# Encoder layer on one core: neighbourhood-attention scores as 64x64 products on the four quarters of the array

## What is computed

```python
s = jnp.einsum('bnqhd,brnchd->bhnqrc', qr, kr).astype(jnp.float32) * scale
bias = jnp.take(col_bias, row_off, axis=1).transpose(0, 2, 3, 1, 4)
s = jnp.where(mask, s + bias.astype(jnp.float32), -jnp.inf)
p = jax.nn.softmax(s.reshape(s.shape[:4] + (-1,)), axis=-1)...
o = jnp.einsum('bhnqrc,brnchd->bnqhd', p, vr)
```

## Time and profile before

| | |
|---|---|
| median of 3 runs | 1249.09 us (1248.29 to 1249.78) |
| profiled execution | 1249.72 us, its span 1248.2 us |
| PE busy | 1172.1 us (94% of the span) |
| DVE, ACT, POOL busy | 649.2, 468.8, 265.6 us |
| granted TensorE clock, mean | 0.977 |

### The profile page before, as it was taken

One profiled execution on the slowest core, in us unless ns is written; L12 is line 12 of the kernel. 1 busy time (PEld: TensorE's weight loads), 2 busy tenths in 40 slices (PEclk: granted clock), 3 DMA queues, 4 the chain that ended last, 5 costly groups with the idle time before them and its releaser, 6 DMA issues.

```text
span 1248.2 us, 18969 instructions
## 1 busy us (share of the span) xinstructions
PE 1172.1 (94%) x6758; PEld 951.7 (76%) x6758; DVE 649.2 (52%) x1244; ACT 468.8 (38%) x982; POOL 265.6 (21%) x384
## 2 busy tenths in 40 slices
PE   6999999999998999999999999999994999999955
PEld 5888888878886777888889788768684888887732
DVE  6332232311114788433367564655466998885247
ACT  6322222200104667211225333445323667674223
POOL 3222222200002223001101000000004233554344
PEclk9999999999998999999999999999996999999978
DMA  9573443763129412442214001732598899979966
GB/s 312 136 239 118 119 159 109 250 158 73 34 56 225 113 27 78 148 158 94 84 25 133 2 1 68 249 121 103 201 346 304 319 386 340 374 291 357 403 263 242
DMA packets 112268, 225.26 MB, mean 180 GB/s; under 512 B 39862, under 2 KB 52158, under 8 KB 112062
## 3 DMA queue, kind: packets, MB, share of 16 engines
q1 hardware_dynamic: 88942, 168.64, 40.8%
q0 software_dynamic: 17856, 43.02, 10.3%
q10 hardware_dynamic: 5392, 12.59, 3.0%
HBM read 180.89 MB, written 69.78 MB: 201 GB/s over the span
## 4 chain that ended last, share of the span: by engine, by line
PE 81%; DVE 5%; DMA 4%; issue 3%; ACT 3%; SPq 2%; POOL 1%; DVEq 0%; ACTq 0%; POOLq 0%
PE bank L565 17%; PE bank L567 17%; PE bank L566 16%; PE bank L2294 5%; PE bank L2070 4%; PE bank L2222 3%; PE bank L2092 3%; PE bank L2260 2%; PE bank L2079 2%; PE bank L2016 2%; PE bank L2231 2%; PE bank L2156 1%; DMA at<-y_mix 1%; PE bank L2280 1%; DVE at L560 1%
## 5 line engine op out<-in xcount | busy, mean ns | idle before, releaser
L565 PE MATMUL bank<-at,at 128*128 128x512 f32 (+1 forms) x1192 | 442.3, 371 | 5.9 <-DVE at L560 3.4
L567 PE MATMUL bank<-at,at 128*128 128x512 f32 (+1 forms) x1192 | 431.8, 362 | 0.0
L566 PE MATMUL bank<-at,at 128*128 128x512 f32 (+1 forms) x1192 | 431.0, 362 | 0.0
L565 PEld LDWEIGHTS bank<-at,at 128*128 128x128 f32 x1192 | 226.1, 190 | 40.6 <-DVE at L560 3.9
L567 PEld LDWEIGHTS bank<-at,at 128*128 128x128 f32 x1192 | 225.7, 189 | 35.2
L566 PEld LDWEIGHTS bank<-at,at 128*128 128x128 f32 x1192 | 226.2, 190 | 32.3
L560 DVE TENSOR_TENSOR at<-at,at 128x1024 fp32r<-128x1024 f32 (+2 forms) x162 | 181.6, 1134 | 86.7 <-ACT at L555 84.0
L555 ACT ACTIVATE at<-at 128x1024 fp32r<-128x1024 f32 (+2 forms) x162 | 154.4, 988 | 146.7 <-DVE at L1529 47.5
L894 POOL TENSOR_TENSOR at<-at 128x1 f32<-128x1 f32 x88 | 24.7, 281 | 501.7 <-ACT at L1259 282.2
L2294 PE MATMUL bank<-at,at 128*128 128x512 f32 x156 | 74.2, 597 | 3.3 <-ACT at L1333 3.3
L1006 POOL DMA_INDIRECT y_tok<-at,at x39 | 39.5, 1013 | 132.5 <-DVE at L1867 95.9
(11 more groups left out here) (214 smaller groups left out, 1409.6 us busy)
## 6 DMA issues: line engine op xcount, KB each, us to landing
at<-in_w_exp_gate SPq DMA_DIRECT2D x39, 512.0 KB
at<-in_w_exp_up SPq DMA_DIRECT2D x39, 512.0 KB
at<-in_w_exp_down SPq DMA_DIRECT2D x39, 512.0 KB
at<-y_tok SPq DMA_DIRECT2D x24, 512.0 KB, 9.7
at<-in_w_in SPq DMA_DIRECT2D x6, 1024.0 KB, 11.3
xT_hi_all<-at POOLq DMA_DIRECT2D x12, 512.0 KB, 3.9
xT_lo_all<-at POOLq DMA_DIRECT2D x12, 512.0 KB, 5.7
at<-xT_hi_all SPq DMA_DIRECT2D x3, 2048.0 KB, 12.0
```

Of the source, the lines that this page charges most:

```text
L565: nc.tensor.matmul(out, w_hi, x_hi, start=(k == 0), stop=False)
L566: nc.tensor.matmul(out, w_lo, x_hi, start=False, stop=False)
L567: last = nc.tensor.matmul(out, w_hi, x_lo, start=False, stop=(k == len(terms) - 1))
```

## The change

- Scores: for each of the two column blocks and each of the two heads one product of 64 queries, 64 rows deep, read straight from `qk`: four products a step instead of two, of the same 256 or 384 columns of keys. The rows used are the head's (half of the array's rows), the output partitions the column block's (half of its columns). A bank now holds one head, and its two halves the two blocks. Only the last product of a bank counts up `s_done`.
- No `q_diag`, no zeroing, no POOL copies, no wait for them. `qk` holds the queries in the order that the products want: the copies out of PSUM write them with a stride of 4 elements (`channel_chunk`). ACT's and DVE's loops over channel tiles are written out, since tiles differ.
- `values`: the loops over block and head swap places; the count of products and their sizes stay.
- Bias tables: a partition now belongs to a column block and needs both heads: 2 heads x 2 kinds x 12 x 32 numbers for each pair. A head takes 16 DMAs instead of 8, each of 2 kinds instead of 3. Heads 0 to 2 are spread ahead of `channel_tiles(1)`, heads 3 to 5 behind it, heads 6 and 7 (their tables take the place of pair 1's, after a memset on POOL) during pair 2, eight DMAs after each of the stores of groups 0 to 3. DVE waits for six heads ahead of pairs 0 to 2, for all eight ahead of pair 3.
- Stores of the attention: two DMAs a group as before, split by column block instead of by head, in runs of 128 numbers instead of 64.
- `FINAL_ORDER` is another permutation; `BY_DVE`'s order comes out the same.

The diff without its context lines (left out too: renumbered counts, the loops written out, the wait for the copies moved):

```diff
-FINAL_ORDER = (0, 4, 1, 5, 2, 6, 3, 8, 7, 10, 9, 11)
+FINAL_ORDER = (0, 4, 5, 1, 6, 2, 8, 3, 10, 7, 11, 9)
...
-        na_bias = at(96, NPAIR, 3, KREL, KC)
-        na_bias_row = at(114, NPAIR, 3, KREL, KC)
+        na_bias = [at(kb, 2, 2, KREL, KC) for kb in (96, 108, 120, 108)]
+        na_bias_row = [at(kb + 6, 2, 2, KREL, KC) for kb in (96, 108, 120, 108)]
...
-        q_diag = [at(132 + 2 * j, 4, 2, QC, QROWS) for j in range(2)]
-        na_o = [at(136 + j, 4, HD) for j in range(2)]
+        na_o = [at(136 + j, 2, 2, HD) for j in range(2)]
...
-        def first_then_loop(eng, n, body):
-            body(0)
-            with eng.Fori(1, n) as i:
-                body(i)
+        def channel_chunk(tile, n, x):
+            out = qk[:, tile, n * CH:(n + 1) * CH]
+            if tile >= NPAIR:
+                return out, x
+            return (out.rearrange("p (g n c r) -> p g r n c", n=4, c=QC, r=QROWS),
+                    x.rearrange("p (g r n c) -> p g r n c", n=4, c=QC, r=QROWS))
...
-            def spread_bias(h):
-                for qr in range(QROWS):
-                    rows = slice((h % 2) * HD + qr, (h % 2 + 1) * HD, QROWS)
-                    src = bias_src[h * QC:(h + 1) * QC]
-                    sp.dma_start(na_bias[rows, h // 2], src[:, :, 3 - qr:15 - qr]).then_inc(bias_here, 16)
-                    sp.dma_start(na_bias_row[rows, h // 2, :, qr:qr + 8], src[:, :, 3:11]).then_inc(bias_here, 16)
+            def spread_bias(h, qr):
+                src = bias_src[h * QC:(h + 1) * QC]
+                for n in range(2):
+                    rows, kinds = slice(n * HD + qr, (n + 1) * HD, QROWS), slice(n, n + 2)
+                    sp.dma_start(na_bias[h // 2][rows, h % 2], src[:, kinds, 3 - qr:15 - qr]).then_inc(bias_here, 16)
+                    sp.dma_start(na_bias_row[h // 2][rows, h % 2, :, qr:qr + 8], src[:, kinds, 3:11]).then_inc(bias_here, 16)
...
-            for h in range(NH // 2):
-                spread_bias(h)
+            for h in range(3):
+                for qr in range(QROWS):
+                    spread_bias(h, qr)
-            for h in range(NH // 2, NH):
-                spread_bias(h)
+            for h in range(3, NH - 2):
+                for qr in range(QROWS):
+                    spread_bias(h, qr)
...
             def store_group(hp, g):
-                for half in range(2):
-                    dst = y_mix[g * GTOK:(g + 1) * GTOK, bass.ds(HALF + (2 * hp + half) * HD, HD)]
-                    sp.dma_start(dst.rearrange("(n q) d -> q n d", n=4),
-                                 na_o[g % 2][half * HD:(half + 1) * HD]).then_inc(na_stored[g % 2], 16)
+                dst = y_mix[g * GTOK:(g + 1) * GTOK, HALF + hp * P:HALF + (hp + 1) * P].rearrange("(s n q) d -> n q s d", s=2, n=2)
+                for n in range(2):
+                    sp.dma_start(dst[n], na_o[g % 2][n * HD:(n + 1) * HD].rearrange("p s h d -> p s (h d)")).then_inc(na_stored[g % 2], 16)
             def head_pair(hp):
...
-            with sp.Fori(1, NPAIR - 1) as hp:
-                head_pair(hp)
+            head_pair(1)
+            sp.wait_ge(pool_made, MADE_LAST_BIAS)
+            for g in range(NKG):
+                store_group(2, g)
+                if g < QROWS:
+                    for h in range(NH - 2, NH):
+                        spread_bias(h, g)
...
-            pool.memset(na_bias_row, MASKED).then_inc(pool_made, 1)
-            for j in range(2):
-                pool.wait_ge(qk_done[j], NH // 2)
-            for j in range(2):
-                pool.memset(q_diag[j], 0.0).then_inc(pool_made, 1)
-            pool.wait_ge(pool_made, MADE_ZERO)
-            for j in range(2):
-                pool.wait_ge(qk_evac_v[j], 2 * (NH // 2))
-                pool.wait_ge(qk_evac_s[j], NH // 2)
-            def head_pair(hp):
-                for g in range(NKG):
-                    pool.wait_ge(s_done, 2 * (NSTEP * hp + max(2 * g - 2, 0)))
-                    for half in range(2):
-                        rows = slice(half * HD, (half + 1) * HD)
-                        q = qk[rows, hp, g * GTOK:(g + 1) * GTOK].rearrange("p (r n c) -> p n c r", n=4, c=QC)
-                        pool.tensor_copy(q_diag[g % 2][rows, :, half], q).then_inc(diag_ready, 1)
-            first_then_loop(pool, NPAIR, head_pair)
+            for hp in range(NPAIR - 1):
+                pool.memset(na_bias_row[hp], MASKED).then_inc(pool_made, 1)
+            pool.wait_ge(s_biased, 2 * 2 * NSTEP)
+            pool.memset(na_bias_row[NPAIR - 1], MASKED).then_inc(pool_made, 1)
-            pool.wait_ge(diag_ready, 2 * NPAIR * NKG)
...
-                        nc.vector.tensor_copy(qk[:, 2 * i + j, n * CH:(n + 1) * CH], bank[3 * j + n][:]).then_inc(qk_evac_v[j], 1)
+                        nc.vector.tensor_copy(*channel_chunk(2 * i + j, n, bank[3 * j + n][:])).then_inc(qk_evac_v[j], 1)
-            with dve.Fori(1, NH // 2 - 1) as i:
+            for i in range(1, NH // 2 - 1):
-            dve.wait_ge(bias_here, 32 + 16 * 3 * QC + 16 * 2 * NH * QROWS)
             def head_pair(hp):
+                dve.wait_ge(bias_here, 32 + 16 * 3 * QC + 16 * 4 * QROWS * (NH if hp == NPAIR - 1 else NH - 2))
                 def scores(s):
-                    bias = (na_bias_row if row_masked else na_bias)[:, hp, kind:kind + 2, first:first + width // KC].rearrange("p n r c -> p n (r c)")
+                    bias = (na_bias_row if row_masked else na_bias)[hp][:, :, kind, first:first + width // KC].rearrange("p h r c -> p h (r c)")
...
-                    o = bank[6 + s % 2][:, 0:P].rearrange("p (n d) -> p n d", n=2)
+                    o = bank[6 + s % 2][:, 0:P].rearrange("p (h d) -> p h d", h=2)
-                    nc.vector.tensor_tensor(na_o[g % 2][:, 2 * (s % 2):2 * (s % 2) + 2], o, r, ALU.mult).then_inc(o_evac, 1)
+                    nc.vector.tensor_tensor(na_o[g % 2][:, s % 2], o, r, ALU.mult).then_inc(o_evac, 1)
...
-                    if s % 2 == 0:
-                        pe.wait_ge(diag_ready, 2 * (NKG * hp + g + 1))
+                    row0 = keys[0] * QROWS
-                        q = q_diag[g % 2][:, block].rearrange("p h c r -> p (h c r)")
-                        row0 = keys[0] * QROWS
-                        k = qk[:, NPAIR + hp].rearrange("p (r c) -> p r c", c=GW)
-                        k = k[:, row0:row0 + QROWS * len(keys), COL_START[block]:COL_START[block] + KC]
-                        nc.tensor.matmul(bank[2 * (s % 2) + n][:, 0:P * len(keys)], q, k, start=True, stop=True).then_inc(s_done, 1)
+                        for half in range(2):
+                            rows = slice(half * HD, (half + 1) * HD)
+                            q = qk[rows, hp, g * GTOK + block * HD:g * GTOK + (block + 1) * HD]
+                            k = qk[rows, NPAIR + hp].rearrange("p (r c) -> p r c", c=GW)
+                            k = k[:, row0:row0 + QROWS * len(keys), COL_START[block]:COL_START[block] + KC]
+                            mm = nc.tensor.matmul(bank[2 * (s % 2) + half][n * HD:(n + 1) * HD, 0:P * len(keys)], q, k, start=True, stop=True)
+                            if n == 1:
+                                mm.then_inc(s_done, 1)
...
-                    for n in range(2):
+                    for half in range(2):
-                            for half in range(2):
-                                rows = slice(half * HD, (half + 1) * HD)
-                                last = nc.tensor.matmul(bank[6 + s % 2][rows, n * HD:(n + 1) * HD],
-                                                        na_pT[s % 2][:, n, k * P + half * HD:k * P + (half + 1) * HD],
+                            for n in range(2):
+                                last = nc.tensor.matmul(bank[6 + s % 2][n * HD:(n + 1) * HD, half * HD:(half + 1) * HD],
+                                                        na_pT[s % 2][:, half, k * P + n * HD:k * P + (n + 1) * HD],
...
```

More of the change, by code:

```diff
@@ L253, in hymba_encoder @@
         pool_made, fill_made = (sem(n) for n in ("pool_made", "fill_made"))
-        MADE_CONST, MADE_BIAS, MADE_ZERO, MADE_ROUTE = 4, 6, 8, 21
+        MADE_CONST, MADE_BIAS, MADE_LAST_BIAS, MADE_ROUTE = 4, 8, 9, 22
         x_sq, x_rs, xs_ready, xt_done = (pair(n) for n in ("x_sq", "x_rs", "xs_ready", "xt_done"))
@@ L267, in hymba_encoder @@
         hi_made, lo_made = sem("hi_made"), sem("lo_made")
-        diag_ready, s_done, s_biased, p_exp, s_rcp = (
-            sem(n) for n in ("diag_ready", "s_done", "s_biased", "p_exp", "s_rcp"))
+        s_done, s_biased, p_exp, s_rcp = (sem(n) for n in ("s_done", "s_biased", "p_exp", "s_rcp"))
         pt_done, pt_evac_s, pt_evac_v, o_done, o_evac = (
@@ L1151, in channel_tiles @@
                     act.wait_ge(qk_done[j], i + 1)
-                    nc.scalar.activation(qk[:, 2 * i + j, CH:2 * CH], bank[3 * j + 1][:], ACT.Copy).then_inc(qk_evac_s[j], 1)
+                    nc.scalar.activation(*channel_chunk(2 * i + j, 1, bank[3 * j + 1][:]), ACT.Copy).then_inc(qk_evac_s[j], 1)
```

(9 more changed lines are left out.)

## The result

The changed kernel takes 1257.29 us (median of 4 runs, 1256.55 to 1258.94), beside 1248.69 for the kernel before in the same comparison: a ratio of 1.0074, with a 95% interval of 1.0055 to 1.0093. So it is slower, by 0.74%. The forecast was 1252.7 us and slower, a loss of 3.6 us; the loss is 8.6.

What follows compares the result with a forecast made beforehand. PE, with 81% of the chain, was taken to bound the kernel; +10.9 -3.2 -3.3 +4.0 -3.3 +2.0 -3.5 makes +3.6 us on the profiled 1249.7, 1253.3, less 0.6 to the median: 1252.7 us, range 1240 to 1266.

Steps and rivals of the forecast that it cites:

- channel stage: Second pair of channel tiles: 48 bias DMAs at 0.64 us delay its weights on SP; +10.9 us with 0.5 for the clock.
- pair 0: Attention's start: PE's wait for POOL's copies shrinks, but values wait for `v_att`; the pair gains only after it, -3.2 us.
- pair 1: Attention: nine of twelve iterations gain from shorter score passes, 5 x 0.27 + 4 x 0.48, so -3.3 us.
- pair 2, wait at pair 3, clock: Last 32 bias DMAs behind stores make SP slower and DVE start pair 3 late, +4.0 us; PE's low clock after, +2.0.
- between attention and final stage: Everything between these stages follows PE and shifts with it; no term of its own.
- final stage: DVE fills its 4.86 us wait for tile 1's root, and tile 9 is last instead of 11: -3.5 us (bounds -4 and 0).
- Rival A: Bias DMAs issue faster, at 0.52 us, and the kernel is faster: 1241.9 us; decides below a spacing of 0.59; chance 0.12.
- B: Score quarters do not all run at once, only two do: passes cost 0.84 us, +0.15 a step, 1268 us; chance 0.10.
- B2: Strict order of score products, only neighbours overlap: five slots, 1.05 us, +0.36 a step, 1275 us; chance 0.04.
- DVE's slack covers the rest of the pace: Attention step: DVE loses 0.27 of its 0.33 us wait, so PE's 0.27 us gain per two-key step comes through.
- Rival C: No cost at the scores' change of shape, and DVE keeps up: about 0 in all, 1248.7 us; chance 0.17.
- Rival D: Final stage gains nothing because `y_tok` loads still fill the DMA engines: +7, so 1256 us; chance 0.15.

Runs made afterwards that it cites:

- e4_order: The kernel before with the new FINAL_ORDER alone: 1245.31 us, ratio 0.9976 to the kernel before.
- e1_lists: The changed kernel with the channel stage's bias DMAs in three lists of 32 instead of two of 48: 1246.30 us, ratio 0.9982 to the kernel before.
- e7_scores_twice: The kernel of e3_both with each score product done twice into the same place: 1251.57 us, ratio 1.0045 to the kernel before.
- e2_late: The changed kernel with pair 3's tables in pair 0's place, their DMAs four at a time behind eight stores in pairs 1 and 2: 1249.05 us, ratio 1.0003.
- e3_both: The changed kernel with the edits of e1_lists and e2_late together: 1238.75 us, ratio 0.9923 to the kernel before.
- e5_values_first: The kernel of e3_both with PE doing the values of step s-2 before transposing step s-1: 1242.28 us, ratio 0.9958 to the kernel before.

## Why the prediction was right, and what its terms missed

The mechanism was right in the main: slower, because two waits for bias DMAs outweigh what the quarters save. The size was not: the loss is more than twice the forecast, and every term missed to the same side. The terms, read from the two profiled executions (span 1257.4 against 1248.2, so +9.2 us, forecast +3.6):

| term | forecast | measured | from |
|---|---|---|---|
| channel stage | +10.9 | +11.0 | first values 400.62 against 389.60 |
| pair 0 | -3.2 | -2.8 | pair 1's scores +8.2 |
| pair 1 | -3.3 | -2.4 | pair 2's scores +5.8 |
| pair 2, wait at pair 3, clock | +6.0 | +6.6 | third scores of pair 3 +12.4 |
| rest of pair 3 | -3.3 | -2.5 | first output product +9.9 |
| between attention and final stage | 0 | +1.8 | end of the last product ahead of the final gap, 1207.3 against 1195.6 |
| final stage | -3.5 | -2.5 | span's end +9.2 |

Of the 5.6 us missing, 2.1 lie in pairs 0, 1 and 3, 0.6 in pair 2 and the wait, 1.8 between the stages, 1.0 in the final stage. Not every term is that sharp. e4_order runs the code of the kernel before up to the final stage, and its timeline of PE has

```profile
380.26 3.75 PE L2070 MATMUL bank<-at,at 128*128 128x256 f32 x8 [3.18 <-POOL at L958]
...
387.20 0.69 PE L2092 MATMUL bank<-at,at 128*64 128x64 f32 x16 [0.28 <-DMA at<-v_att]
...
412.46 1.99 PE L2070 MATMUL bank<-at,at 128*128 128x256 f32 x8
```

So with the same code the attention starts 2.0 us earlier and pair 0 is 2.1 us shorter (32.20 against 34.26): the first two terms are good to some 2 us each, and what pair 0 gains is not shown. Pairs 1 to 3 repeat within 0.02 us.

**Channel stage: right, in part by luck.** 48 DMAs at 0.64 us, though each moves less, as the equal times of the two kinds before had said. PE starts at 289.13 (forecast 289.6). The third pair's weights stayed hidden, as forecast (the prediction's 321.5 should be 314.7 + 6.4 = 321.1). The clock cost more than the 0.5 us: 0.50 was granted over six us, where 0.72 was before. PE's second pair of tiles starts 9.9 us later (forecast 10.4), and the stage's last product ends 11.2 later (390.24 against 379.04), so the clock took some 1.3: two misses that nearly cancel. The wait ahead of the attention's first scores then shrank from 3.18 us to 1.68, so they start 9.7 us later. Rival A needed a spacing under 0.59 and is out; e1_lists puts the whole term at 11.5 us.

**The score passes: right; the step was set by something else.** Forecast 0.42 us for two passes, 0.43 measured by e7_scores_twice; rivals B and B2 (0.84 and 1.05 us) are out. For the change of shape and the weights that show I had charged 0.28, and 0.59 - 0.43 = 0.16 stands there. The Trainium skill (TensorEngine Tiling (Array Packing), Key Properties) has the array drain at each change of mode, and the trace agrees with a pause there: 0.16 to 0.19 us at each of the three changes, beyond the passes at 0.105 us for 128 columns. By that alone a step would be 1.79 us, better than the forecast 1.84. The step that failed is "DVE's slack covers the rest of the pace": DVE did, but behind it ACT's two exponentials and its copy did not, and the transpositions waited for them, so a step is 1.91. The timeline of the changed kernel shows which of ACT's instructions came last:

```profile
431.79 0.36 ACT L1165 ACTIVATE at<-bank 128x256 f32<-128x256 f32 x1
...
432.22 0.42 PEld L2072 LDWEIGHTS bank<-at,at 128*128 128x128 f32 x4 [0.48 <-ACT at L1158]
```

PE's row names the exponential, but `transpose_p` also waits for ACT's copy of the transpositions before, out of the same bank, and that copy ends at 432.15, 0.07 us ahead of them, as in each of the four such steps of pair 1. ACT does it behind both exponentials. With three key groups a step is 2.46 (forecast 2.51). Rival C, a step still cheaper, did not come: the pause is there, and ACT sets the step.

**A pair gains 2.44 us and not 3.3.** Comparing pair 1 step by step with the kernel before: the four inner two-key steps gain 0.71 us together (1.08 expected) and the eleventh, which I had put at 0.27, 0.11, so two-key steps are 0.53 short. The four from the seventh on gain 1.74 (1.92 expected), since the first transpositions of three key groups, at 438.5, come 0.96 us after the last weights of the scores instead of 0.60: they wait for ACT. And the head, which I had given nothing, loses 0.16: its third scores come 3.01 us after the first instead of 2.85.

**Pair 2: the wait was there and larger, its clock smaller.** DVE starts pair 3 at 36.8 us after pair 2's first scores (488.58 - 451.78), where I had 34.7: the first store came at 8.2 and not 7.3, and two of the 32 DMAs took 1.3 us instead of 0.6. That is +6.1 instead of +4.0. The clock took back some 0.9 instead of 2.0: 0.55 us more from DVE's start to the third scores, 0.3 in the step after. The granted clock was 0.72 over six us, much as I had taken, but part of that stretch had been PE waiting for ACT, and slower products fill such a wait first: in e2_late, with the same code and no stop, PE waits 0.57 us for ACT there.

**Final stage: right in kind.** 2.5 us in this execution, 3.0 by e4_order, 3.5 forecast. Rival D is out.

**Between attention and final stage** I had nothing, and the executions disagree: +1.8 here, +1.6 in e2_late, -0.2 in e1_lists, -0.3 in e3_both, with the same code there. So it isn't shown to be of the change, and it makes a fifth of this execution's loss. I can't say what sets it.

What stays open is how much of a pair this wait would give back if ACT's copy lay ahead of the exponentials or on another engine, which no run tried; e5_values_first shows only that its order on PE doesn't do it.

## What to carry to other kernels

Count the DMAs that a new layout issues before counting what its products save: here each bias DMA cost its queue 0.64 us whatever it moved, and 16 more of them ahead of one weight load cost more than the quarters gave in four pairs. Put such transfers where the queue has an idle stretch before their first reader, in lists no longer than the work that covers them; moving them alone turned 1.0074 into 0.9923. When one part of a step is made shorter, follow the chain of the engines that feed the next part as well as the one with the visible slack.

## What the runs showed of the hardware beside this

- Four quarters of the array, two row halves by two column halves, run at once with float32 operands: four more products of 256 columns, eight passes, cost 0.43 us, which is the time of two passes one after another (0.42 by the price of 0.105 us for 128 columns). The Trainium skill (TensorE: Matmul & The Clock Gate, Part 3) has products start and end in program order; with a product's two passes one behind the other the eight would need five slots, 1.05 us, as the prediction's B2 says, so either the rule doesn't hold the next product up here or the passes lie in another order, and no run tells which.
- A copy out of PSUM that writes with a stride of 4 elements takes longer. In the two lists by source, for DVE's and for ACT's copies (minimum, median and maximum in ns):

```profile
L1449 DVE COPY at<-bank x16: 678/876/1081, 271.3 to 390.9; 128x512 f32<-128x512 f32 x16
```

```profile
L1141 ACT ACTIVATE at<-bank x8: 597/837/1096, 271.3 to 390.3; 128x512 f32<-128x512 f32 x8
```

  Before, all of them took 0.60 to 0.69 us. The query tiles are strided and the key tiles not, so 1.08 and 1.10 against 0.68 and 0.60. It lay under products, as forecast.
